# An eighth seven-product pair in each half of w_down, with the up block sums made by ScalarE's negation and an accumulating DMA

## What is computed

```python
h = rmsnorm(x, g_ffn_pre[l])
ff = (jax.nn.silu(h @ w_gate[l]) * (h @ w_up[l])) @ w_down[l]
x = x + rmsnorm(ff, g_ffn_post[l])
```

## Time and profile before

| | us |
|---|---|
| median of 3 runs (lowest, highest) | 1198.8 (1198.7, 1198.92) |
| the profiled execution | 1198.35 |
| its span | 1196.6 |
| PE busy in the span | 1183.2 |
| DVE busy | 997.0 |
| ACT busy | 690.6 |
| POOL busy | 81.4 |

### The profile page before, as it was taken

One profiled execution on the slowest core, in us unless ns is written; L12 is line 12 of the kernel. 1 busy time (PEld: TensorE's weight loads), 2 busy tenths in 40 slices (PEclk: granted clock), 3 DMA queues, 4 the chain that ended last, 5 costly groups with the idle time before them and its releaser, 6 DMA issues.

```text
span 1196.6 us, 16463 instructions
## 1 busy us (share of the span) xinstructions
PE 1183.2 (99%) x5727; PEld 992.7 (83%) x5727; DVE 997.0 (83%) x1334; ACT 690.6 (58%) x930; POOL 81.4 (7%) x87
## 2 busy tenths in 40 slices
PE   8999999999999999999999999999999999999997
PEld 7888888888888888888888888888888888888885
DVE  6656777877786755879999999999999789979997
ACT  5654676474654744665666566555656455555553
POOL 1000110000000000001110110111010011001100
PEclk9999999999999999999999999999999999999999
DMA  8656867767786656565575666657566765655654
GB/s 314 206 159 158 226 172 153 182 144 190 182 190 170 226 186 194 171 236 195 198 234 184 205 212 221 200 192 238 185 201 210 246 199 192 217 201 188 231 170 149
DMA packets 124596, 237.23 MB, mean 198 GB/s; under 512 B 8312, under 2 KB 24960, under 8 KB 123392
## 3 DMA queue, kind: packets, MB, share of 16 engines
q1 hardware_dynamic: 122784, 231.05, 61.9%
q0 software_dynamic: 1760, 5.51, 1.8%
HBM read 229.97 MB, written 4.20 MB: 196 GB/s over the span
## 4 chain that ended last, share of the span: by engine, by line
PE 92%; DVE 4%; DMA 2%; ACT 1%; issue 1%; SPq 0%; DVEq 0%; ACTq 0%
PE bank L1787 90%; DMA raw<-in_w_in 2%; DVE w_lo L1132 1%; DMA resid<-in_x 1%; PE bank L2064 1%; DVE w_lo L1618 0%; PE bank L1792 0%; PE bank L1981 0%; ACT w_hi L711 0%; DVE more_lo L1618 0%; DVE raw L1635 0%; DVE v_sb L1259 0%; DVE gT L1346 0%; DVE h L1159 0%; DVE resid L1780 0%
## 5 line engine op out<-in xcount | busy, mean ns | idle before, releaser
L1132 DVE TENSOR_TENSOR w_lo<-raw,w_hi 128x1024 fp32r<-128x1024 f32 x172 | 209.1, 1223 | 120.4 <-ACT w_hi L711 120.0
L711 ACT ACTIVATE w_hi<-raw 128x1024 fp32r<-128x1024 f32 x172 | 180.5, 1058 | 162.0 <-PE bank L1787 149.6
L1787 PE MATMUL bank<-hT,w_hi 128*128 128x512 f32 x768 | 271.1, 396 | 0.4 <-DVE w_lo L1132 0.4
L1787 PE MATMUL bank<-w_hi,h2T 128*128 128x512 f32 x778 | 253.4, 391 | 0.0
L1787 PE MATMUL bank<-hT,w_lo 128*128 128x256 f32 x768 | 214.6, 279 | 0.0
L1787 PEld LDWEIGHTS bank<-hT,w_hi 128*128 128x128 f32 x768 | 144.0, 187 | 32.7 <-DVE w_lo L1132 0.7
L1787 PEld LDWEIGHTS bank<-w_hi,h2T 128*128 128x128 f32 x778 | 146.1, 188 | 30.0
L1787 PE MATMUL bank<-w_lo,h2T 128*128 128x512 f32 x379 | 147.5, 389 | 0.0
L1787 PEld LDWEIGHTS bank<-hT,w_lo 128*128 128x128 f32 x768 | 145.0, 189 | 0.0
L1615 DVE TENSOR_TENSOR w_lo<-raw,w_hi 128x1024 fp32r<-128x1024 f32 x108 | 131.0, 1228 | 12.6 <-ACT w_hi L1022 12.5
L1618 DVE TENSOR_TENSOR w_lo<-raw,w_hi 128x1024 fp32r<-128x1024 f32 (+1 forms) x130 | 135.2, 1075 | 2.3 <-ACT w_hi L1036 1.7
(11 more groups left out here) (265 smaller groups left out, 1819.5 us busy)
## 6 DMA issues: line engine op xcount, KB each, us to landing
raw<-in_w_in SPq DMA_DIRECT2D x63, 1024.0 KB, 11.0
raw<-in_w_down SPq DMA_DIRECT2D x88, 512.0 KB, 4.9
raw<-in_w_up SPq DMA_DIRECT2D x80, 512.0 KB, 3.9
raw<-in_w_gate SPq DMA_DIRECT2D x80, 512.0 KB, 4.7
raw<-in_w_out SPq DMA_DIRECT2D x16, 1024.0 KB, 5.1
raw<-in_w_gate SPq DMA_DIRECT2D x4, 1024.0 KB, 5.2
raw<-in_w_up SPq DMA_DIRECT2D x4, 1024.0 KB, 6.7
raw<-raw POOLq DMA_DIRECT2D x9, 256.0 KB, 5.8
```

The source lines that it names most:

```text
L711: act.activation(part_of(w_hi, rnd, s), src, ACT.Copy).then_inc(hi_done, 1)
L1132: dve.tensor_tensor(part_of(w_lo, rnd, s), raw_sub(rnd, s)[1], part_of(w_hi, rnd, s).bitcast(F32), ALU.subtract).then_inc(lo_done, 1)
L1787: return pe.matmul(out_, lhsT, rhs, start=start, stop=stop, skip_group_check=True)
```

## The change

Each plan of w_down gets an eighth S, and they stand at other places. All t3 of w_down are made as the fourth of an FFN group was: ACT's negation of the S unit's b12 stands behind its high part of piece 0 of the R unit before, POOL's instruction becomes the issue of the accumulating DMA, and ACT's piece 2 and DVE's t2 wait for `t3_moved` in place of `t3_ready`.

```diff
-DOWN = Plan("RRRSRRSRSRRSRSRRSRSRRR")
-LAST_HALF = Plan("RRRSRSRRSRSRRSRSRSRRRR")
+DOWN = Plan("RRRSRSRRSRSRRSRSRRSRSR")
+LAST_HALF = Plan("RRRSRSRSRSRSRSRSRSRRRR")
...
-def last_of_group(i, n):
+def sum_moved(i, n):
 
-    return down_half(i) is None and n == SEVEN[-1]
+    return down_half(i) is not None or n == SEVEN[-1]
+
+def moved_sums(i, n):
+
+    if down_half(i) is not None:
+        return FF_GROUPS - 1 + d_of(down_half(i), n)
+    return i
...
+            def up_sum_moved(i, n):
+
+                q = chunk_of(i, n)
+                pool.wait_ge(up_turned, moved_sums(i, n))
+                pool.dma_start(raw[:, q, 0:512], raw[:, q, 512:1024], accum_op=ALU.add).then_inc(t3_moved, 16)
...
             for half in range(2):
                 for n in DOWN_SEVEN[half]:
-                    up_sum_of(FF_GROUPS + half, n)
+                    up_sum_moved(FF_GROUPS + half, n)
...
                 elif piece == 2:
-                    if last_of_group(i, n):
-                        act.wait_ge(t3_moved, 16 * i)
+                    if sum_moved(i, n):
+                        act.wait_ge(t3_moved, 16 * moved_sums(i, n))
...
+            def turn_up(i, n):
+
+                q = chunk_of(i, n)
+                act.wait_ge(raw_up[q], up_arrived(i, n))
+                act.activation(raw[:, q, 0:512], raw[:, q, 0:512], ACT.Copy, scale=-1.0).then_inc(up_turned, 1)
...
                     unit_hi(i, odd, plan, m)
+                    n, piece = plan.pieces[m]
+                    if n + 1 in DOWN_SEVEN[half] and piece == 0:
+                        turn_up(i, n + 1)
...
                     dve.wait_ge(lo_done, ff_base(i) + m)
-                    if last_of_group(i, n):
-                        dve.wait_ge(t3_moved, 16 * i)
+                    if sum_moved(i, n):
+                        dve.wait_ge(t3_moved, 16 * moved_sums(i, n))
```

More of the change, by code:

```diff
@@ L141, in sums_index @@
     return len(SEVEN) * i + (SEVEN.index(n) - len(SEVEN))
-def last_of_group(i, n):
-    return down_half(i) is None and n == SEVEN[-1]
+def sum_moved(i, n):
[4 more added lines that the diff above has]
+    return i
 def up_sums_before(i, n):
-    if down_half(i) is not None:
-        return 3 * (FF_GROUPS - 2) + 2 + HALF_SEVEN * down_half(i) + DOWN_SEVEN[down_half(i)].index(n)
     return 3 * i + (SEVEN.index(n) - 3)
@@ L683, in _ @@
                 up_sum_of(i, SEVEN[2])
-                q = chunk_of(i, SEVEN[3])
-                pool.wait_ge(up_turned, i)
-                pool.dma_start(raw[:, q, 0:512], raw[:, q, 512:1024], accum_op=ALU.add).then_inc(t3_moved, 16)
+                up_sum_moved(i, SEVEN[3])
             first_pairs_sums(FF_GROUPS - 1)
@@ L1051, in ff_group @@
                     if m == FULL.base[SEVEN[2]] - 1 and plan is FULL:
[L1052 to L1055, removed]
+                        turn_up(i, SEVEN[3])
                     if m == 0 and first:
```

## The result

| | before | after |
|---|---|---|
| median of 5 runs, us | 1198.8 (1197.99 to 1200.46) | 1204.88 (1204.26 to 1206.91) |
| profiled execution, us | 1198.35 | 1204.85 |
| its span, us | 1196.6 | 1203.1 |

The ratio is 1.0054, with a 95% interval of 1.004 to 1.0069: the change makes the kernel 6.1 us slower. 1199.2 was forecast, and the range ended at 1202.7.

What follows compares the result with a forecast made beforehand. PE was taken as the bound, busy 1183.2 of 1196.6 us. Matmuls -1.36, second-half loop +1.2 and first half +0.5 sum to +0.4, from 1198.8 to 1199.2; range from 1197.4, with 0.2 for measurement, to 1202.7.

Steps and rivals of the forecast that it cites:

- The gain of the matmuls: In w_down two units turn from R to S, six matmuls fewer on PE: -1.36 us.
- The loop: In w_down's S, R rows, t14 to next t14 through ACT, POOL's DMA and DVE: 10.74 us against PE's 10.20.
- L: Time from POOL's issue of the accumulating DMA to its landing, taken as 5.7 us from nine earlier DMAs.
- case B: Rival: w_down's DMAs land later than in most FFN groups, loop paid seven times; 1202.7 at 6.2, 1208.3 at 7.0; chance 0.20.
- 7 x L - 39.5: Approximate sum of all terms in us for L from 5.5 up; each tenth of a microsecond of L costs 0.7 us.
- The loads beside it look alike: Ground for using FFN-group landings in w_down: its 1 MB load would be issued at about the DMA's moment.
- its second reason: DVE holding the port shared with POOL delays descriptor writing; one 1.22 us DVE instruction more gives L = 6.9, 1208 us.
- Case A: Rival: w_down's DMAs land fast enough, L of 5.2 or less, whole 1.36 us gained, 1197.4; chance 0.12.
- Case C: Rival: DVE's work alone becomes the bound; 10.35 us a step, six steps lose 0.9, under the 2.0 reserve; part of forecast.
- a reserve: In w_down POOL's sums hold DVE up 1.1 us; removing them gains nothing by itself but leaves slack for the loop.
- the 0.5 us put down for its unit 5: First half of w_down: PE waits at unit 5, short of reserve since unit 3 starts with PE waiting; +0.5 us.

Runs made afterwards that it cites:

- Four kernels without the loop's waits: New plans on the kernel before without t3 sums, 0.9986; the change with earlier negation, 0.9987; with loads 1.6 or 0.7 us later, both 0.9984.
- the last experiment: The change with SP's 1 MB loads issued 1.6 us later, 1196.39 us, or 0.7 us later, 1196.48 us; both ratio 0.9984 to the kernel before.

## Why the prediction was wrong

- **The gain of the matmuls was right.** -1.36 us was forecast. Four kernels without the loop's waits came out at 0.9984 to 0.9987, 1.5 to 2.1 us under the kernel before, with intervals that hold 1.36 us (0.9989); from the first S to the last PE takes 1.2 to 1.3 us less in them.
- **The loop was right, link by link.** It was put at 5.04 us + L, and with L = 6.6 the trace shows 11.62. PE's waits are at piece 0 for `d_ops`, as said, first at unit 5 of the first half. They come before five S of the second half, by about 1.1 to 1.3 us each, which is the sign that the prediction gave for its case B. One label of the rows is wrong: the sum of POOL at 1096.76 is not that of unit 5, whose t2 had started at 1095.21, but the next in POOL's list, for unit 8. The hold-up of DVE beside it stands as read.
- **L was wrong, and it is the term that failed.** It was put at 5.7, from the FFN groups' rows, and in the alternating row of w_down it was 6.6. With 6.6 the prediction's own line, 7 x L - 39.5, gives +6.7 against the +6.1 measured (+6.5 in the spans). The step that let it pass is the sentence "The loads beside it look alike": in the groups the load came 1.3 us before and the next 1.0 after, in w_down one at the same moment. The offset had been worked out (2.93 us behind t14's end for both) and was then read as no difference. Moving the load by 0.7 and 1.6 us moved L by 2.3 and 3.3.
- **The range was too short upward.** It ended at L = 6.2, 0.2 above the later eight issues, though L was multiplied by seven and none of the nine had been issued in w_down; the largest, 7.0, should have been inside.
- **Case B was what happened**, with 0.20 and its price right; its second reason was not the cause, as the last experiment shows. Case A named the other end: L of 3.3 exists, but only where no load starts beside the DMA.
- **Not priced:** what the plans would do with POOL's sums. Case C counted DVE's work without them (10.35 us a step) and found room for it, as the new plans with no sums show. With POOL's sums the same count gives 11.45 (11.31 measured), and the plans alone lose 4.7 us, 1202.84 against 1198.11. The prediction called POOL's 1.1 us a reserve; in an unbroken row of S, R it is a loss.
- **The first half** lost more than the 0.5 us put down for its unit 5. With L - 5.2 as its price and the 6.3 us that its DMA took it would be 1.1; PE lost 1.0 there (984.19 to 985.43, less one matmul). Another 0.2 is at its last S, which starts 10.39 us behind the S before in place of 10.20.

What stays open: whether the earlier negation would hold with L at 6.6, since it shortened L too; and why a load that is issued at the same moment delays the DMA. In the trace's packets the DMA's first one comes 1.4 us behind its issue with no load beside it, and 2.8 to 3.1 behind both in w_down with a load at the same moment and in the FFN groups with one 1.3 us before. In w_down its packets then take 3.0 to 3.4 us from first to last, without one mostly 1.5 to 2.2. With the load 0.7 us behind, it is the load that waits: its first packet comes about 2.1 us behind its issue in place of 1.0. All this was only observed. Nor do the neighbours' issues settle L alone: the first of the FFN groups' nine took 7.0 us with the same loads beside it, at the same distances, as the eight that took 5.6 to 6.0.

## What to carry to other kernels

Where a transfer stands in a loop with engines' work, add up the loop and compare it with the bound engine's period; if they are close, the latency counts once for each turn, and the range must be that many times as wide. Take a DMA's latency from rows with the same neighbours in time, and not from its own earlier issues alone: here the same 256 KB took, in the median, 3.3, 4.3, 5.7 or 6.6 us by where the loads beside it stood. Such a loss can be repaired by order alone: a negation three instructions earlier, or a load 0.7 or 1.6 us later, each made a kernel faster than both, 1196.4 to 1196.6 us.

## What was not expected of the hardware

- The accumulating DMA of 256 KB within SBUF landed 3.3 us after its issue with the next 1 MB load 1.6 us behind, 4.3 with it 0.7 behind, and 6.6 with it at the same moment. Putting the load off by 0.7 us brought the DMA's landing forward by 2.3. With one load 1.9 us before it and the next 0.4 behind (units 8, 13 and 18 of the first half in the change), it landed after 7.1 to 7.6.
- The Trainium skill, page "DMA: Bandwidth & Descriptors", section "Anatomy of one DMA — SWDGE (gpsimd) path", fits a DMA of this size at an estimated 2.6 us. The shortest landing in these runs is 3.2 us, with no load issued within 2.4 us; here the measurement decides.
- A DVE instruction of 0.28 us took 1.26 beside one of POOL's sums, one of 0.69 took 1.78, and one of 1.22 took 2.14 (in the kernel before at 1109.72): 0.9 to 1.1 us more, whatever the length of the DVE instruction.
